# A tuned fp32 network on one core: a first threshold group ahead of the first values, norm sums added on GpSimd, last output rows joined in pairs

## The reference

```python
for i in range(2):                                   # first_block
    shift1, scale1, gate1, shift2, scale2, gate2 = mod(i)     # silu(c) @ ada_w[i] + ada_b[i]
    h = rms_norm(x, norm_mix[i]) * (1 + scale1) + shift1
    y = mla_mixer(h) if i == 0 else dilated_mixer(h)
    x = x + gate1 * y
    h = rms_norm(x, norm_mlp[i]) * (1 + scale2) + shift2
    x = x + gate2 * (square(relu(h @ mlp_w1[i])) @ mlp_w2[i])
# second_block
y_a, y_b = rg_lru(...) * gelu(gate), chunk_attention(...)
x = x + concat(rmsnorm(y_a), rmsnorm(y_b)) @ w_out
x = x + memory_cross_attention(rmsnorm(x), rmsnorm(mem))
x = rmsnorm(x + peer(rmsnorm(x)))                    # 16384 experts, top 16 of 8 heads
```

## Time and profile before

| | |
|---|---|
| median of 3 runs | 2017.81 us (2015.99 to 2019.18) |
| profiled execution, its own time | 2018.96 us |
| its span in the trace | 2017.2 us |
| PE busy | 1966.6 us of the span |
| DVE, ACT, POOL busy | 1410.9, 1143.8, 311.6 us |
| mean granted TensorE clock of the span | 0.992 |

### The profile page before, as it was taken

One profiled execution on the slowest core, in us unless ns is written; L12 is line 12 of the kernel. 1 busy time (PEld: TensorE's weight loads), 2 busy tenths in 40 slices (PEclk: granted clock), 3 DMA queues, 4 the chain that ended last, 5 costly groups with the idle time before them and its releaser, 6 DMA issues.

```text
span 2017.2 us, 34914 instructions
## 1 busy us (share of the span) xinstructions
PE 1966.6 (97%) x14224; PEld 1824.1 (90%) x14224; DVE 1410.9 (70%) x2546; ACT 1143.8 (57%) x1935; POOL 311.6 (15%) x333
## 2 busy tenths in 40 slices
PE   8998999999999989999999999999999999999997
PEld 5798999999888879999989999999999998888886
DVE  6777765887776667656756478999986765555554
ACT  5865543556667545544755464457677754444444
POOL 0010000000000000001100000038868940000000
PEclk9999999999999999999999999999999999999999
DMA  9465787346444327666435355554444445555553
GB/s 358 158 209 179 245 285 245 120 141 238 155 151 142 116 89 239 196 178 230 136 114 166 123 169 172 179 177 147 157 148 156 139 156 189 189 189 190 189 190 117
DMA packets 97743, 356.25 MB, mean 177 GB/s; under 512 B 11104, under 2 KB 11232, under 8 KB 97200
## 3 DMA queue, kind: packets, MB, share of 16 engines
q1 hardware_dynamic: 84240, 305.04, 45.3%
q0 software_dynamic: 12624, 48.08, 7.3%
q10 hardware_dynamic: 720, 0.91, 0.1%
HBM read 352.94 MB, written 1.05 MB: 175 GB/s over the span
## 4 chain that ended last, share of the span: by engine, by line
PE 90%; DVE 4%; ACT 3%; DMA 2%; issue 1%; SPq 1%; DVEq 0%; ACTq 0%; POOLq 0%
PE psum L589 24%; PE psum L591 24%; PE psum L590 24%; PE psum L582 17%; PE psum L596 2%; DVE wl L2088 1%; DMA first<-in_ada_w 1%; SPq L3099 1%; ACT work L1409 1%; ACT wh L1421 0%; DMA araw<-in_ada_w 0%; ACT na L1409 0%; DMA memx<-in_mem 0%; DMA raw<-in_mla_w_kvb 0%; DVE xc L2068 0%
## 5 line engine op out<-in xcount | busy, mean ns | idle before, releaser
L2088 DVE TENSOR_TENSOR wl<-raw,wh 128x1024 fp32r<-128x1024 f32 (+1 forms) x566 | 689.8, 1222 | 410.8 <-ACT wh L1421 409.4
L1421 ACT ACTIVATE wh<-raw 128x1024 fp32r<-128x1024 f32 (+1 forms) x566 | 593.7, 1050 | 429.1 <-PE psum L591 390.4
L589 PE MATMUL psum<-peer_hh,wh 128*128 128x256 f32 x1024 | 296.3, 289 | 0.0
L590 PE MATMUL psum<-peer_hl,wh 128*128 128x256 f32 x1024 | 290.3, 284 | 0.0
L591 PE MATMUL psum<-peer_hh,wl 128*128 128x256 f32 x1024 | 290.3, 283 | 0.0
L590 PE MATMUL psum<-wl,csh 128*128 128x512 f32 x512 | 201.9, 394 | 0.0
L589 PE MATMUL psum<-wh,csh 128*128 128x512 f32 x512 | 201.8, 394 | 0.0
L591 PE MATMUL psum<-wh,csl 128*128 128x512 f32 x512 | 201.8, 394 | 0.0
L589 PEld LDWEIGHTS psum<-peer_hh,wh 128*128 128x128 f32 x1024 | 194.5, 190 | 0.0
L590 PEld LDWEIGHTS psum<-peer_hl,wh 128*128 128x128 f32 x1024 | 194.3, 190 | 0.0
L591 PEld LDWEIGHTS psum<-peer_hh,wl 128*128 128x128 f32 x1024 | 194.3, 190 | 0.0
(11 more groups left out here) (453 smaller groups left out, 4861.3 us busy)
## 6 DMA issues: line engine op xcount, KB each, us to landing
raw<-in_mlp_w SPq DMA_DIRECT2D x128, 512.0 KB, 4.2
raw<-in_eu SPq DMA_DIRECT2D x128, 512.0 KB, 3.4
raw<-in_ev SPq DMA_DIRECT2D x128, 512.0 KB, 3.4
araw<-in_ada_w POOLq DMA_DIRECT2D x76, 512.0 KB, 4.7
raw<-in_dil_qk SPq DMA_DIRECT2D x48, 512.0 KB, 4.0
raw<-in_dil_v SPq DMA_DIRECT2D x24, 512.0 KB, 3.5
raw<-in_w_in SPq DMA_DIRECT2D x16, 512.0 KB, 3.5
raw<-in_w_query SPq DMA_DIRECT2D x16, 512.0 KB, 3.5
```

Source lines behind the costliest of these rows:

```text
L589: e.matmul(o, l[0], r[0], start=start, stop=False, skip_group_check=loose)
L590: e.matmul(o, l[0], r[1], start=False, stop=False, skip_group_check=loose)
L1421: e.activation(b.wh[v % NSPLIT][:, 0:cols], b.raw[v % NRAW][:, 0:cols], ACT.Copy).then_inc(S.hi, 1)
L2088: e.tensor_tensor(b.wl[v % NSPLIT][:, 0:cols], b.raw[v % NRAW][:, 0:cols], b.wh[v % NSPLIT][:, 0:cols].bitcast(F32), ALU.subtract).then_in ...
```

## The change

**Ends of the mixers.** The two mixers' last two output units (6 and 7) are multiplied column by column (`rows_end`, which the cross attention had already), so that out tiles 0 to 5 are complete before PE is done with the two; the first two pairs of sums stand in between, two pairs behind. In MLA the units before move back by one place against the attention steps.

**Sums.** In `mlp0`, `mlp1`, `out2` and `mo` GpSimd adds the squares up, and PE takes one or two sums where it took eight; `ya` and `yb` have two for four. The norms `out2` and `n6` take place one to three units later. The odd tiles' lows of `n6` move from DVE to GpSimd, and ACT makes an unrounded copy (`cross_odd`) for them.

**Distance tables.** They are made beside the second product of `mlp0`; their three transfers move to its start. The first threshold group stands ahead of the first values on PE, and every later group moves up.

```diff
-    outer = {12: 0, 13: 1, 14: 2, 15: 3, 16: 4, 17: 5, 18: 6, 19: 7}
+    outer = {13: 0, 14: 1, 15: 2, 16: 3, 17: 4, 19: 5}
...
-    return out
+    return out + [("hi", 6), ("lo", 6), ("wo", 6), ("wo", 7)]
...
 def cross_order():
-    out = [("unit", "w_mem_v", 4), ("tiles", None, 0), ("total", None, None), ("unit", "w_mem_v", 5),
-           ("tiles", None, 4), ("unit", "w_mem_v", 6), ("root", None, None), ("unit", "w_mem_v", 7)]
+    out = [("unit", "w_mem_v", 4), ("tiles", None, 0), ("unit", "w_mem_v", 5),
+           ("tiles", None, 4), ("unit", "w_mem_v", 6), ("unit", "w_mem_v", 7), ("total", None, None)]
     for i in range(8):
         out.append(("unit", "w_q_mem_2", i))
         if i == 0:
+            out.append(("root", None, None))
+        if i == 1:
             out.append(("columns", None, None))
...
         out.append(("query", c, None))
-        if c == 0:
+        if c == 3:
             out += [("root", None, None)]
-        if c == 2:
+        if c == 4:
             out.append(("columns", None, None))
-        if c in (2, 3, 4, 5):
-            out += [("tile", 2 * c - 4, None), ("tile", 2 * c - 3, None)]
-        if c == 6:
+        if c in (4, 5, 6, 7):
+            out += [("tile", 2 * c - 8, None), ("tile", 2 * c - 7, None)]
+        if c == 8:
             out.append(("tile", 8, None))
...
-        for k in range(nk):
-            pe.wait_ge(S.act, at[tag, "sq", int(k >= nk // 2)])
-            mm(ps[:, 0:256], ones, q3[:, k, :], k == 0, k == nk - 1, mark=(tag, "sum") if k == nk - 1 else None)
+        pe.wait_ge(S.pool, at[tag, "added"])
+        for k in range(nk // 2):
+            mm(ps[:, 0:256], ones, q3[:, k, :], k == 0, k == nk // 2 - 1, mark=(tag, "sum") if k else None)
         give(tag, "sum", sem=S.act, key=(tag, "ms"))
...
+    def tile_sums(tag, m):
+
+        ps = take(tag, "total")
+        pe.wait_ge(S.pool, at[tag, "added", 6])
+        mm(ps[:, 0:256], ones, m.sbf[:, 0:256], True, False)
+        pe.wait_ge(S.act, at[tag, "square", 7])
+        mm(ps[:, 0:256], ones, m.rbf[:, 768:1024], False, True, mark=(tag, "squares", 7))
+        give(tag, "total", sem=S.act, key=(tag, "ms"))
+
+    def pair_sums(tag, pairs):
+
+        ps = take(tag, "total")
+        pe.wait_ge(S.pool, at[tag, "added", 3])
+        mm(ps[:, 0:256], ones, pairs[0][:, 0:256], True, True, mark=(tag, "squares", 3))
+        give(tag, "total", sem=S.act, key=(tag, "ms"))
...
-    def rows_end(tag, name, k, x, ring):
...
-            if c in (5, 7):
+            if ring is not None and c in (5, 7):
                 square_sums(tag, c // 2 - 2, ring)
         for c2 in range(4):
             give(tag, c2, sem=S.dve, key=(tag, "out", c2))
+        if ring is not None:
+            square_sums(tag, 2, ring)
+            square_sums(tag, 3, ring)
...
-                pe.wait_ge(S.dve, at["mla", "out", i])
-                rows_unit("mla_o", "mla_w_o", i, sp(m.hh, i), i == 0, i == 7)
-        for c2 in range(4):
-            square_sums("mla_o", c2, m.ring)
+                if i < 6:
+                    pe.wait_ge(S.dve, at["mla", "out", i])
+                    rows_unit("mla_o", "mla_w_o", i, sp(m.hh, i), i == 0, False)
+                elif i == 7:
+                    pe.wait_ge(S.dve, at["mla", "out", 7])
+                    rows_end("mla_o", "mla_w_o", 6, [sp(m.hh, 6), sp(m.hh, 7)], m.ring)
...
-                if c and q == 1:
-                    tile_sum((tag, 2), c - 1, m.rbf)
...
         if layer == 0:
-            tile_sum((tag, 2), 7, m.rbf)
+            tile_sums((tag, 2), m)
...
         side = chain(bias(0), bias(1))
+        next(side)
+        next(side)
...
+            x = [[m.o[:, k, 0, :], m.o[:, k, 1, :]] for k in (i, min(i + 1, 7))]
+            if i < 6:
+                pe.wait_ge(S.dve, at["dil", "out", i])
+                rows_unit("dil_o", "dil_w_o", i, x[0], i == 0, False)
+            elif i == 6:
+                pe.wait_ge(S.dve, at["dil", "out", 7])
+                rows_end("dil_o", "dil_w_o", 6, x, m.work)
...
-                for c2 in range(4):
-                    square_sums("out2", c2, x.xcf)
+                pair_sums("out2", x.pairs)
...
-        query_at = lambda k: (S.dve, ("n6 gain", "lo", k))
+        query_at = lambda k: (S.pool if k % 2 else S.dve, ("n6 gain", "lo", k))
...
-                if i == 0:
-                    square_sums("mo", 2, b.cross.ring)
-                    square_sums("mo", 3, b.cross.ring)
+                if i == 3:
+                    pair_sums("mo", b.cross.pairs)
...
-    def square(tag, c2, ring, after):
+    def square(tag, c2, ring, after, added=False):
...
-        if c2 >= 2:
+        if c2 >= 2 and not added:
...
-        r = ring[:, (c2 % 2) * 512:(c2 % 2) * 512 + 512]
+        r = ring[c2] if added else ring[:, (c2 % 2) * 512:(c2 % 2) * 512 + 512]
...
-            ac.wait_ge(S.pe, at[tag, "squares", k - 4])
+            ac.wait_ge(S.pool, at[tag, "added", max(1, k - 4)])
...
         for c2 in range(4):
+            if c2 == 3:
+                unit("mla_w_o", 7)
...
+    def bias_tables(s):
+
+        m = b.dil
+        if s == 6:
+            ac.wait_ge(S.dve, at["tab diff"])
+            act(m.tabs[:, 0, 0, :], m.ot[:, 0:192], ACT.Copy, mark=("tabs", "hi"))
+        elif s == 11:
+            ac.wait_ge(S.dve, at["tabs"])
+            act(m.tabs[:, 1], m.tabs[:, 0].bitcast(F32), ACT.Copy, scale=0.5, mark=("tabs", "half"))
+            ac.wait_ge(S.dve, at["keys"])
+            sides.append(chain(bias(0), bias(1)))
+            next(sides[0])
...
+            if layer == 0:
+                bias_tables(s)
...
-            for k in (2 * c2, 2 * c2 + 1):
+            ac.wait_ge(S.dve, at["mo", "out", c2])
+            act(m.odd[:, c2 * 256:c2 * 256 + 256], b.xs3[:, 2 * c2 + 1, :], ACT.Copy,
+                scale=vc(b, "ffn", 2 * c2 + 1), mark=("odd", c2))
+            for k in (2 * c2 + 1, 2 * c2):
                 tile_high("n6 gain", ("mo", "out", c2), k, vc(b, "ffn", k), x.hh)
-            square("mo", c2, m.ring, ("mo", "out", c2))
+
+    def squares(c):
+        for c2 in (2 * c, 2 * c + 1):
+            square("mo", c2, b.cross.pairs, ("mo", "out", c2), True)
...
+                if i < 2:
+                    squares(i)
...
+        rows_residual("mla_o", u + 1, lambda c: b.mod[:, 16 + c:17 + c])
+        unit("mla_w_o", 7)
...
@@ -2587,6 +2618,30 @@
             yield
         yield
 
+    sides = []
+
+    def bias_tables(s):
+
+        m = b.dil
+        pI = m.ot[:, 384:705].bitcast(I32)
+        if s == 5:
+            ve.wait_ge(S.tables, 16)
+            tt(m.ot[:, 0:192], m.ot[:, 0:192], m.ot[:, 192:384], ALU.subtract, mark="tab diff")
+            ve.wait_ge(S.pos_rows, 16)
+            ts(pI[:, 320:321], pI[:, 320:321], -1, None, ALU.bitwise_xor)
+            own()
+            tt(pI[:, 0:320], pI[:, 0:320], pI[:, 320:321].broadcast_to([128, 320]), ALU.add)
+        elif s == 7:
+            ve.wait_ge(S.act, at["tabs", "hi"])
+            own()
+            tt(m.tabs[:, 0, 1, :], m.ot[:, 0:192], m.tabs[:, 0, 0, :].bitcast(F32), ALU.subtract, mark="tabs")
+            cp(m.pF, pI[:, 0:320])
+            own()
+            ts(m.key, m.pF[:, 0:64], cc(b, "lo"), 0.5, ALU.subtract, ALU.add, mark="keys")
+        elif s == 10:
+            sides.append(chain(bias(0), bias(1)))
+            next(sides[0])
+
...
+        side = sides[0]
+        next(side)
...
+        unit("dil_w_o", 7)
...
-                    for k in (2 * c2 - 2, 2 * c2 - 1):
-                        tile_low("n6 gain", k, vc(b, "ffn", k), x.hh)
+                    tile_low("n6 gain", 2 * c2 - 2, vc(b, "ffn", 2 * c2 - 2), x.hh)
                 yield
+            tile_low("n6 gain", 6, vc(b, "ffn", 6), x.hh)
             ahead(UNIT_OF["w_query_2", 1] - AHEAD)
-            for k in (6, 7):
-                tile_low("n6 gain", k, vc(b, "ffn", k), x.hh)
 
         lows = after()
...
-    def phase(name):
+    def phase(name, left=None):
+
         at["phase", "pool", name] = n[0]
+        if left:
+            left()
...
+    def own():
+        po.wait_ge(S.pool, n[0])
+
+    def add_tiles(tag, m, every=0):
+
+        total = m.sbf[:, 0:256]
+        for k in range(1, 7):
+            if every:
+                tick(8 if k == 1 else 4, every)
+            po.wait_ge(S.act, at[tag, "square", k])
+            own()
+            tt(total, m.rbf[:, (k % 4) * 256:(k % 4) * 256 + 256], total if k > 1 else m.rbf[:, 0:256], ALU.add,
+               (tag, "added", k))
+
+    def add_pairs(tag, pairs):
+
+        for c2 in range(1, 4):
+            po.wait_ge(S.act, at[tag, "square", c2])
+            own()
+            tt(pairs[0], pairs[0], pairs[c2], ALU.add, (tag, "added", c2))
+        own()
+        tt(pairs[0][:, 0:256], pairs[0][:, 0:256], pairs[0][:, 256:512], ALU.add, (tag, "added", 3))
+
     def mla():
 
...
                 tt(z, z, m.tmp[:, 0:256], ALU.mult, ("in2", "scaled", c2))
+        for name, sq in (("ya", m.xcf), ("yb", m.work)):
```

(64 more changed lines are left out.)

80 lines of the change are left out of this document (18 added, 62 removed).

## The result

The changed kernel took 2004.76 us (median of 4 runs, 2004.4 to 2005.0), the kernel before 2017.26 (4 runs, 2015.99 to 2019.18): ratio 0.9937, 95% interval 0.992 to 0.9954. That is 12.5 us less where 16.0 were forecast. The time lies inside the range (1996 to 2008.5) and inside the likeliest case's own range (1998.5 to 2005).

A forecast was written before the change was run, and what follows sets the result against it. The prediction took PE's own work as the bound (busy 97% of the span). Its terms summed to 16.05 us saved, from a median of 2017.8 to 2001.8 us, range 1996 to 2008.5.

The forecast's parts named there:

- likeliest case: Whole kernel: the forecast itself, 2001.8 us, with its own range 1998.5 to 2005 and a chance of 0.61.
- B: `mlp0` and `mlp1`: seven and six sums fewer on PE, 3.0 and 2.6 us saved, GpSimd's adds hidden in DVE's idle time.
- A: End of MLA: unit 6 to the last sum takes 10.45 us instead of 12.29, 1.8 us saved.
- E: End of the dilated mixer: same form and kind of waits as MLA's end, 1.85 us saved (1.2 to 2.2).
- D: Tables and first group at the dilated mixer's start: group fills most of the 3.68 wait, 0.8 us saved (-1.5 to 2.1).
- That leaves 0.8: Dilated mixer's start: 2.1 us gained by order, less 1.3 booked for half clock behind a new gap of 3.1.
- The rival that this would gain 5.2: Dilated mixer's start: second group doesn't wait, 5.2 us saved in place of 0.8, giving 1997.4; chance 0.10.
- C: `ya` and `yb`: four sums fewer on PE, 1.7 us saved, bounds 0.5 to 1.7.
- F: `out2`: seven sums fewer, 3.0 us, less 0.8 for GpSimd's contention with DVE: 2.2 saved (1.6 to 3.0).
- G: `mo` and peer's start: seven sums fewer, 3.0 us, less 0.4 for a later `wl` and 0.5 contention: 2.1 saved.
- two slow stretches take back what the change gives: Rival: new gaps at dilated and peer starts bring full-length slow stretches, about 2 us more each: 2006; chance 0.10.
- Contention: Rival: GpSimd's adds in `out2` and `mo` slow DVE, 5.6 us reaching PE instead of 1.3: 2006; chance 0.13.

The follow-up runs named there:

- the second profile: The changed kernel run and profiled once more with no edit: 2005.76 us, ratio 0.9947 against the kernel before run beside it (2016.38 us).

## Why the prediction came out as it did

**B, the sums in the layers: right.** 93.93 - 90.78 = 3.15 for seven in layer 1, 0.45 each, where both profiles have the same rate; 0.43 was booked. (In the first profile, with its layer at 0.120, 2.1 is left.) The 2.6 of layer 2 came with 1.2 that was not booked (121.47 - 117.68 = 3.8): PE's two waits for `wl` in `w_in_2`, 0.32 at 940.92 and 1.03 at 948.39 us, have become one of 0.41. No run shows why. GpSimd's adds there cost nothing, as the run without them shows.

**A, the end of MLA: right in its place, incomplete around it.** From the start of the joined units (147.43) to the last sum's end (156.56 + 1.13 = 157.69) are 10.3 us; 10.45 was forecast, 12.29 stood there. But the attention steps in front became a little longer: PE's waits for `na` are 1.9 in two before, 2.1 in three in the changed kernel, 2.9 in six in the kernel with the early comparison. Between that kernel and the two profiles of before, all three with a slow stretch somewhere from 91 to 97 us, the stage differs by only 0.7 and 0.9 (76.19 against 76.91 and 77.07). So up to 1.7 to 2.1 of the measured 2.4 and 2.8 goes with that stretch, which both profiles of before have and one of twelve after; the nine with the same MLA order and without it took 74.09 to 75.50, so some of it is spread. It follows PE's wait of 1.5 for `na` at 91 us, which all profiles have, and the orders of PE, ACT and DVE are the same up to about 120 us, in both kernels: nothing that the change moves on these engines lies ahead of it. No run shows a cause of this gain in the change; why the stretch is gone stays open.

**E, the end of the dilated mixer: right, then given back.** 301.13 - 299.53 = 1.6 (1.85 booked); the 298.07 of the second profile has a slow stretch of 3.4 us at 682 where the others have 6.8. But the next product, which has the same work and the same wait ahead, costs 1.2 more (94.19 against 93.00), and 0.7 to 2.1 more in all eight profiles with that end and no extra matmuls: its slow stretch starts earlier and lasts 6.8 us, and where the layer runs at 0.120, 1.0 of it is that. With the extra matmuls it takes 92.55, and 93.52 at 0.120. The same happened at layer 1 in some profiles (94.15) and not in others (92.74). The forecast held the clock behind an unchanged wait to be unchanged; this cost had no term.

**D, the tables and the first group: wrong, sign and all.** The step that failed is "That leaves 0.8". Measured are -0.65 and -1.9. The mechanism was named: the second group waits for its comparison. The wait was forecast at 3.1 and is 2.7 in the second profile and in three variants with the same start; it is 1.4 in the first profile and in the run with extra matmuls ahead of the layers, where a slow unit ahead of it took up the rest. What was wrong was the price of the clock. From the 2.1 that the order alone was to gain, 1.3 was booked for it; from 2.1 down to -0.65 and -1.9 are 2.75 and 4.0. Unit 0 was taken to run at the full clock behind the first group; there were 3.4 + 6.8 us of slow stretches in one profile, 10.2 in the other. The first group's 24 matmuls of 128 columns, with 1.06 idle behind, did not keep the clock up ahead of unit 0 in two profiles of the nine with this start. The rival that this would gain 5.2 needed an order that the change doesn't have. With the second unit ahead of the second group the gain is 4.0.

**C: right on paper, partly lost.** `w_out` is 0.86 shorter, two sums. Of the other two, 0.36 arrived where both profiles have a slow stretch of 3.4 us in this stage (96.41 to 96.06), since a new wait of 0.36 for a `wl` came behind, in the first profile 0.37 at 1000.29 us; it is there with adds of one column too, so it isn't theirs. The first profile took 94.53: it has no slow stretch there, which is worth 1.5 more and comes and goes between profiles of the same kernel:

```profile
982.10:985.30 3.20, 3.20 (x17) 3.20 (x17) 3.20 (x5) 0.62 (x1) 1.03 (x1) 0.50 0.53 175
```

```profile
975.00:990.00 15.00, 13.17 (x108) 12.82 (x108) 13.51 (x17) 9.74 (x16) 3.14 (x3) 1.00 0.56 165
```

The first row is the second profile's, the second row the first's.

**F: the mechanism right, its size off.** Booked 3.0 less 0.8 of contention; the contention cost 1.5 (22.67 against 21.20), and 1.8 was gained. The price per quarter was not too low: the four lows lost 3.18 - 1.67 = 1.5 us beside about four quarters, 0.4 each. What was too low was the share of this that reaches PE: all of it, and not about a fifth of the 3.8 at most.

**G: right.** 77.37 - 75.14 = 2.23, 2.1 booked, with waits of 0.62 and 1.16 for lows of DVE where one of 2 for a low of GpSimd was forecast. PE has no wait for `skT` in the changed kernel, as counted; in one variant, which leaves this place as it is, it waited 1.39 us.

**The rivals.** That two slow stretches take back what the change gives (0.10, 2006) is closest to what happened, though one of its places was the second layer and not the peer's start. Contention (0.13) had 1.5 us in it, not 5.6.

**The sum: inside the range, partly by luck.** In the first profile the stages give 14.0 us where 16.0 were booked. Against the forecast stood D and the slower first product of layer 2 (1.5 and 1.2) and the layer at 0.120 (2.0); for it stood two slow stretches that the profiles of before have and this one doesn't, at 91 and at 990 us (about 1.7 and 1.5), and 1.2 in `w_in_2`. None of the last three was forecast. The medians say 12.5 and, in the second comparison, 10.6, and the 2005.76 measured there lies above the likeliest case's own range.

## What to carry to other kernels

A gap on a matmul engine has two prices, its length and the half clock behind it, and work moved into it may lower the first and leave the second. Compare the order in which the next steps wait, not only whether the gap is filled: one unit moved by one place was worth about 5 us here (4.7 and 5.9), more than the move of the group ahead of the values, which alone lost 1.2 and 2.4 (88.62 against 89.77 and 91.00). Where nothing useful is at hand, matmuls that nobody reads, on data that is there, kept the clock. Take stages and not whole times to judge an edit of 1 or 2 us: many stages agreed to 0.02 us between two profiles of a kernel where the clock was the same, while the runs of one kernel spread over up to 7.7. Take two profiles at the least: a stage of one profile alone may hold 1.5 us of clock that the next one doesn't have.

## What the hardware showed unexpectedly

- A feed-forward layer's fp32r matmuls of 128x128 by 256 columns came every 0.1187 us in some executions and every 0.120 in others, for the whole layer of some 190 us, with the granted clock at 1.00 in both: 90.78 against 91.80 us for the same second product. Of the four profiles with extra matmuls ahead of both layers only the last has layers at 0.120, and neither profile of the kernel before has it; what brings it isn't shown.
- `mix_hl`, a scalar-tensor-tensor with two operands in SBUF, took 0.80 us each beside GpSimd's adds (3.18 for four) and 0.42 alone (1.67 for four). The Trainium skill, GPSIMD Engine Reference, section 1, names instructions with two SBUF inputs as those that contend, and the rows agree.
- A slow stretch may begin inside the idle wait (159.0 to 161.3 above reads 0.50 with no matmul in it), so the first matmuls behind it are slow from the start.
